# Two strips of weights multiplied together: the first strip goes three k tiles alone, the second catches up

## The reference, cut to what matters

```python
def conv_ffn(h, w_up, w_dw, b_dw, w_down):          # w_up 1024 x 5632, w_down 2816 x 1024
    u = h @ w_up
    u = causal_dwconv(u, w_dw, b_dw)                # 3 taps
    gate, val = jnp.split(u, 2, axis=-1)
    return (jax.nn.silu(gate) * val) @ w_down
...
for l in range(DEPTH):                              # DEPTH = 2
    h = rmsnorm(x, g_mix[l])
    ...
    hk = rmsnorm(x, g_kv)                           # second mixer only
    kvf = hk @ w_kvf                                # keys, values, forget gates
    p = h @ w_in_b[l - N_A]                         # queries, memory queries
    ...
    x = x + jnp.concatenate([mix, mem_o], axis=-1) @ w_out[l]
    x = x + conv_ffn(rmsnorm(x, g_ffn[l]), w_up[l], w_dw_f[l], b_dw_f[l], w_down[l])
```

## Time and profile before

| | |
|---|---|
| median of 3 runs | 2591.67 us (2590.96 to 2592.72) |
| the profiled execution | 2593.99 us, its span 2592.2 us |
| mean granted TensorE clock | 0.989 of full |
| TensorE matmuls busy | 2499.6 us, 96% |
| TensorE weight loads busy (beside the matmuls) | 1954.3 us, 75% |
| VectorE busy | 1532.7 us, 59% |
| ScalarE busy | 1053.2 us, 41% |
| DMA | 262.43 MB, mean 101 GB/s |

### The profile page before, as it was taken

How to read it: one execution, slowest core, us unless ns; L and a number is a source line. 1 busy time by engine, 2 the same in 40 slices (tenths; PEclk the granted TensorE clock), 3 DMA queues, 4 the chain that set the end, 5 groups by cost and what they waited for, 6 DMA issues and landing times.

```text
span 2592.2 us, 30725 instructions
## 1 busy us (share of the span) xinstructions
PE 2499.6 (96%) x12218; PEld 1954.3 (75%) x12218; DVE 1532.7 (59%) x2298; ACT 1053.2 (41%) x1628; POOL 76.4 (3%) x154
## 2 busy tenths in 40 slices
PE   7999999999998999999999999999999989999999
PEld 5667777777865787777778578888879657788887
DVE  5996778776455477768657654333364765533334
ACT  5345333334455343323554734222244673522223
POOL 2000000000000000000000000000000000000000
PEclk9999999999999999999999999999999999999999
DMA  5123356453212346555222023333223112233231
GB/s 173 52 82 97 115 178 187 149 178 105 80 52 74 98 123 185 172 159 176 78 82 82 1 66 98 98 87 93 85 78 98 50 49 67 81 98 93 90 86 57
DMA packets 328094, 262.43 MB, mean 101 GB/s; under 512 B 13659, under 2 KB 312863, under 8 KB 327953
## 3 DMA queue, kind: packets, MB, share of 16 engines
q1 hardware_dynamic: 310176, 205.08, 26.8%
q0 software_dynamic: 15696, 54.34, 6.5%
q10 hardware_dynamic: 2080, 1.05, 0.2%
HBM read 258.32 MB, written 2.12 MB: 100 GB/s over the span
## 4 chain that ended last, share of the span: by engine, by line
PE 85%; DVE 6%; ACT 4%; DVEq 2%; issue 1%; DMA 0%; ACTq 0%; PEldq 0%; PEld 0%
PE ps L416 55%; PE ps L434 7%; PE ps L430 7%; PE ps L438 6%; PE ps L1431 2%; PE ps L2037 1%; DVE wL L382 1%; PE ps L1445 1%; PE ps L1469 1%; PE ps L2548 1%; DVEq L994 1%; DVE tmpA L1004 1%; DVEq L1006 1%; ACT tmpB L1530 1%; DVEq L1903 1%
## 5 line engine op out<-in xcount | busy, mean ns | idle before, releaser
L382 DVE TENSOR_TENSOR wL<-raw,wH 128x2048 fp32r<-128x2048 f32 (+1 forms) x185 | 415.2, 2244 | 126.7 <-ACT wH L368 120.6
L368 ACT ACTIVATE wH<-raw 128x2048 fp32r<-128x2048 f32 (+1 forms) x185 | 345.5, 1869 | 242.1 <-PE ps L416 101.3
L416 PE MATMUL ps<-hH,wH 128*128 128x512 f32 x1656 | 429.2, 401 | 2.8 <-DVE gate L918 1.8
L416 PE MATMUL ps<-hH,wL 128*128 128x512 f32 x1656 | 425.1, 398 | 0.0
L416 PE MATMUL ps<-hL,wH 128*128 128x512 f32 x1656 | 424.7, 398 | 0.0
L416 PEld LDWEIGHTS ps<-hH,wH 128*128 128x128 f32 x1656 | 308.4, 188 | 88.9 <-issue 14.0
L416 PEld LDWEIGHTS ps<-hH,wL 128*128 128x128 f32 x1656 | 308.9, 188 | 83.2 <-issue 10.8
L416 PEld LDWEIGHTS ps<-hL,wH 128*128 128x128 f32 x1656 | 309.1, 188 | 77.1 <-issue 4.5
L1030 DVE TENSOR_TENSOR tmpB<-ps,tmpB 128x512 f32<-128x512 f32 x44 | 30.4, 691 | 229.9 <-PE ps L416 229.9
L967 ACT ACTIVATE tmpA<-ff_up,cols 128x512 f32<-128x512 f32 x88 | 67.0, 809 | 239.4 <-DVEq L994 239.4
L434 PE MATMUL ps<-gH,wL 128*128 128x512 f32 x480 | 149.6, 401 | 4.7 <-DVE wL L382 4.7
(11 more groups left out here) (401 smaller groups left out, 3254.7 us busy)
## 6 DMA issues: line engine op xcount, KB each, us to landing
raw<-w_up SPq DMA_DIRECT2D x132, 512.0 KB, 5.2
mod_ring<-w_mod POOLq DMA_DIRECT2D x96, 512.0 KB, 4.3
raw<-w_down SPq DMA_DIRECT2D x32, 1024.0 KB, 5.5
raw<-w_gate SPq DMA_DIRECT2D x44, 512.0 KB, 4.0
raw<-w_down SPq DMA_DIRECT2D x16, 768.0 KB, 4.6
raw<-w_in_even SPq DMA_DIRECT2D x9, 1024.0 KB, 5.2
raw<-w_out SPq DMA_DIRECT2D x8, 1024.0 KB, 5.3
raw<-w_in_odd SPq DMA_DIRECT2D x16, 512.0 KB, 4.6
```

The costliest lines, as they stand in the source:

```text
L368: last = act.activation(wH[:, st.part, 0:st.size], raw[:, st.slot, 0:st.size], ACT.Copy)
L382: last = dve.tensor_tensor(wL[:, st.part, 0:st.size], raw[:, st.slot, 0:st.size], wH[:, st.part, 0:st.size].bitcast(F32), ALU.subtract)
L416: last = pe.matmul(dst, left, right, start=(t == 0 and k == 0), stop=(t == 2 and k == self.kt - 1))
```

## The change

`Run` gets a number `lead`. With it, `multiply_gated` does the first `lead` k tiles for the first strip's two tiles alone, then the same k tiles for the second strip's two, and from there on all four tiles as before. Gates are still asked once for each k tile, at the first use. `lead=3` is given to every down run of the four feed-forwards and to `ahead`; all other runs have 0.

```diff
-            def __init__(self, form, count, kt, pieces, take, width=STRIP, tokens=SEQ, gain=None, order=None):
-                self.form, self.kt, self.take = form, kt, take
+            def __init__(self, form, count, kt, pieces, take, width=STRIP, tokens=SEQ, gain=None, order=None, lead=0):
+                self.form, self.kt, self.take, self.lead = form, kt, take, lead
...
-                for i, k in enumerate(order[:together]):
-                    gate.high(pe, k)
-                    for tile in tiles:
+                lead = self.lead if len(pair) > 1 else 0
+                first, second = pair[0].tiles, pair[-1].tiles
+                rounds = [(first, i, True) for i in range(lead)] + [(second, i, False) for i in range(lead)]
+                for some, i, new in rounds + [(tiles, i, True) for i in range(lead, together)]:
+                    k = order[i]
+                    if new:
+                        gate.high(pe, k)
+                    for tile in some:
                         if i == 0:
                             pe.wait_ge(bank_read[tile.bank].sem, tile.free)
                             pe.wait_ge(weights_high.sem, START + tile.strip.n + 1)
                         high(tile, k)
-                    for tile in tiles:
+                    for tile in some:
                         if i == 0:
                             pe.wait_ge(weights_low.sem, START + tile.strip.n + 1)
                         weight_low(tile, k)
                     if i:
-                        gate.low(pe, order[i - 1])
-                        for tile in tiles:
+                        if new:
+                            gate.low(pe, order[i - 1])
+                        for tile in some:
                             low(tile, order[i - 1])
...
-                                  last if first + count == FT else TakeResidual(gain, aside=aside, step0=n * (D // STRIP)))
+                                  last if first + count == FT else TakeResidual(gain, aside=aside, step0=n * (D // STRIP)), lead=3)
...
-                    gain=lambda s: of_kv if s else of_q)
+                    gain=lambda s: of_kv if s else of_q, lead=3)
```

## The result

The changed kernel takes 2579.06 us (median of 4 runs, 2576.91 to 2582.14), the kernel before 2591.67 (median of 4, 2590.96 to 2592.72). The two medians are 12.6 us apart. The ratio estimated from the runs is 0.9947, 95% interval 0.9935 to 0.9959, which makes 13.7 us, between 10.6 and 16.8. Forecast were 2578.2 us and 13.5. On a second occasion the same two kernels gave 2578.41 and a ratio of 0.9946 (0.9932 to 0.9960). The profiled execution took 2580.59 us, 2578.8 of it span, 13.4 less than the span before.

What follows compares the result with a forecast made beforehand. TensorE was taken as the bound, its matmuls busy 96% of the span; stall and clock savings of 5.51 + 3.83 + 4.17 = 13.5 us at A, B and C took 2591.67 to 2578.2 us, range 2573 to 2586.5.

Steps and rivals of the forecast that it cites:

- fourth rounds: A pair's 33rd matmul, first of the fourth k tile; undisturbed, the 32 matmuls ahead of it take 7.47 us.
- B: Pair start at 629 us, `ahead` of the second mixer: no stall left, fourth round 3.83 us earlier.
- C: Pair start at 984 us, first-third down run, second feed-forward: no stall left, fourth round 4.17 us earlier.
- A: Pair start at 337 us, first-third down run, first feed-forward: 0.34 us stall left, fourth round 5.51 us earlier.
- the excess: Time over 7.47 us to the fourth round at A, B and C: 5.95, 4.11 and 4.56 us, mainly stall and clock.
- rival 1: Stalls go, but stretches at 1.2 GHz stay or come elsewhere: gain 7.5 us, 2584.2 us; chance 10%.
- The residual wait: Stall of 0.34 us left at A for the second strip's wL; full clock assumed, else up to 2.71 us lost.
- The reserve of VectorE: Margin by which VectorE's idle time exceeds the gain when the pair's tiles end: 0.24 us behind A, 0.50 behind C.
- Rival 2: VectorE takes the gain back behind A and C; only B's 3.8 us is left, 2587.8 us; chance 5%.
- The order for nothing: The new order itself costs nothing: value 0, ends +-10 ns on each of 416 matmuls, +-4 us.
- Rival 3: Order itself costs, banks being rewritten after two matmuls: at 50 ns each +7.3 us, 2599 us; chance 3%.
- rival 4: Second strip's weights come as much later as they are wanted later, VectorE's queue following TensorE: 2591.7 us; chance 5%.

Runs made afterwards that it cites:

- e1: Kernel before, with lead=3 only in `ahead` of the second mixer (B): 2590.39 us, ratio 0.9989.
- e2: Kernel before, with lead=3 only in the first-third down runs of the two convolution feed-forwards (A and C): 2583.44 us, ratio 0.9967.
- e4: Kernel before, with useless matmuls (10 at A and C, 8 at B) ahead of the wait for the second strip's wL: 2589.08 us, ratio 0.9988.
- e6: Changed kernel with lead=2 instead of 3 in all thirteen pairs: 2585.04 us, ratio 0.9972 to the kernel before.
- e3: Kernel before, with lead=3 only in the ten down runs that waited for no weights: ratio 1.0006.
- e5: Changed kernel with lead=1 instead of 3 in all thirteen pairs: 2593.22 us in one run, beside 2592.67 for the kernel before.
- e10: Kernel before, with six useless matmuls ahead of the four pairs whose source comes from a norm: 2589.07 us, ratio 0.9983.
- e9: Changed kernel run once more, unaltered: 2578.41 us, ratio 0.9946 to the kernel before.
- e8: Changed kernel with six useless matmuls ahead of the four pairs whose source comes from a norm: 2575.52 us, ratio 0.9935 to the kernel before.
- e11: The kernel of e8 run a second time: 2576.21 us, ratio 0.9935 to the kernel before.

## Why the prediction was right

**The places.** Forecast as fourth rounds earlier by 5.51, 3.83 and 4.17 us; measured 5.37, 4.11 and 4.32. At B the small gap of 0.28 us among the first four matmuls was carried over, and it went away; at C, of 0.39 about 0.24 remained. At A the second strip's wL came 4.68 us behind the start instead of 4.64, and the two matmuls behind the wait took 0.10 us more than two steps: that is the 0.14 missing there. (The profile's 0.22 us of wait is not to be held against the forecast 0.34, which was reckoned from starts of rows; by these it was 0.38.) The fourth round was forecast 7.8 to 8 us behind each start, and B and C came sooner, at 7.47 and 7.71. The kernels with one part each (e1, e2) show the places work apart from each other.

**The stall and the clock.** The split of the excess in 7.14 us of stall and 5.99 of clock is the step that needed a test. e4 takes the clock's part alone and finds 4.6 to 5.7 us of it at the three places (by whether A's slow stretch is a short or a long one), though only 3.1 (0.8 to 5.4) in the whole time; rival 1 (the slow stretches stay) falls, with all three windows at 1.00. The term was a little large: 2.71 us at A is what this one trace had, and two other traces of the old order have a shorter stretch there and a fourth round at 12.4. The Trainium skill's price for a throttled stretch (TensorE: Matmul & The Clock Gate, Terms) made 3.4 us of the window at A, idle time included; the fill won 2.6 there, so the rows were the better source.

**The residual wait.** Chosen was full clock behind 0.34 us. That holds, and e6 shows a wide margin in its one trace: 1.64 us still left the clock alone. The waits of 1.69 us in the earlier trace rows say less than the forecast took from them: the kernel before has four, and behind three of them a slow stretch came, not behind one of two, and sparse matmuls stand ahead of them, which is not so at A.

**What is late next.** The reserve of VectorE was forecast at 0.24 us behind A and 0.50 behind C; it is 0.33 and 0.34. Rival 2 (VectorE takes the gain back) needed it to be negative. From A to B the two traces differ by 0.01 us.

**The order for nothing.** Ends of +-4 us were kept for it; e3 has 1.0006 (0.9997 to 1.0015) and the same 233 ns. Rival 3 falls. So does rival 4: the split of wL starts 2.34 us behind the pair as before (2.30), and its end does not follow TensorE.

**The sum** was right within what can be measured, partly since errors cancelled: the places gave 0.3 us more than forecast, and the rest of the span 0.4 less, by slow stretches that the sum had at nothing. Later stages were to lie 5.5, then 9.3, then 13.5 us earlier; they lie 4.6 at the start of B, 8.2 at the start of C and 13.4 at the end. The mean clock rose from 0.989 to 0.991, the low end of the forecast, with slow stretches elsewhere that came and went.

## What to carry to other kernels

When two consumers share rounds and the second one's input is late, let the first run ahead by just the matmuls that cover the delay. Read the delay from the start of the pair, not from the wait: here 4.7 us against 233 ns a matmul, and a lead of 18 matmuls to the late operand. A stall of TensorE of some 2 us amid dense matmuls cost nearly twice its length here, so look at the pace of the matmuls behind it too; where the stall can't be removed, matmuls of no use in it gave the second half back.

## What the runs showed of the hardware

- Behind waits of 2.0 to 2.8 us in the midst of dense matmuls a stretch at 1.2 GHz followed in all 15 cases (the kernel before, e1, e2, e3, e5, e10). Behind 1.64, 1.28 and 0.91 us, in one trace, none did. Behind the norm waits of 1.69 us, with sparse operations ahead of them, it came in 25 of 40 cases, at some starts and not at others of the same trace. No run here shows what sets the border.
- A slow stretch cost 1.6 or 2.7 us of matmul time at A, B and C. The spread of one kernel's runs goes with the clock: the changed kernel's first four took 2576.91 and 2577.52 us at a mean granted clock of 0.993, 2580.59 at 0.991 and 2582.14 at 0.990, with nothing changed. Which stretches make this spread is not shown: its two traces (the first one and e9's) have them in the same places. The two traces of the kernel that e8 and e11 ran differ in the sparser stages (granted clock from 185 to 205 us 0.83 and 0.91, from 685 to 698 us 1.00 and 0.87).
- Matmuls whose result is never used kept the clock up as well as real ones: with them in the waits it was 1.00 in the windows around A, B and C (e4) and the four norm starts (e11).
